# The norm's factor behind the products of the second block's stages

## The reference, cut to what matters

```python
def rms_norm_2(x, g):
    y = xf * lax.rsqrt(jnp.mean(xf * xf, axis=-1, keepdims=True) + EPS)
    return (y * g.astype(jnp.float32)).astype(x.dtype)

def second_block(x, ...):
    for l in range(DEPTH):
        h = rms_norm_2(x, norm1_g[l])
        z = h @ w_in[l]
        (cq, ckv, kpe, gq, gk, gv, glr, gr, su, gates) = split_in(z)
        ...
        x = x + merged @ w_out[l]
        h2 = rms_norm_2(x, norm2_g[l])
        x = x + jnp.square(jax.nn.relu(h2 @ w_ff1[l])) @ w_ff2[l]
```

## Time and profile before

| | |
|---|---|
| median of three runs | 2344.2 us (2341.02 to 2348.77) |
| profiled execution | 2345.54 us, span 2343.5 us |
| PE busy | 94% |
| PE weight loads | 89% |
| DVE busy | 71% |
| ACT busy | 60% |
| DMA, mean | 168 GB/s |

### The profile page before, as it was taken

The page is one execution under the profiler, slowest core; times in us unless marked ns, Lnnn a source line. Parts: engine busy times, 40 slices in busy tenths (PEclk is TensorE's granted clock), DMA queues, the critical chain, the costliest instruction groups (busy, mean ns, idle before and its releaser), DMA issues.

```text
span 2343.5 us, 42543 instructions
## 1 busy us (share of the span) xinstructions
PE 2200.8 (94%) x17524; PEld 2089.8 (89%) x17524; DVE 1656.4 (71%) x2998; ACT 1417.2 (60%) x2205; POOL 200.2 (9%) x178
## 2 busy tenths in 40 slices
PE   2989999999998999999999999899999989899999
PEld 2979899999998898999998987789999987799999
DVE  5898778678769887785879663647687663656653
ACT  2578887466546888854763557564543548564542
POOL 0000000022000000000231111000030111000000
PEclk9999999999999999999999999999999999999999
DMA  7555556567755564574655323245566323344553
GB/s 281 189 161 181 165 198 219 179 207 231 238 192 174 157 198 162 195 228 147 205 176 167 126 84 99 94 149 164 189 184 187 117 66 110 107 153 144 195 189 129
DMA packets 110593, 394.64 MB, mean 168 GB/s; under 512 B 12320, under 2 KB 13888, under 8 KB 110272
## 3 DMA queue, kind: packets, MB, share of 16 engines
q1 hardware_dynamic: 96768, 343.47, 45.3%
q0 software_dynamic: 11904, 43.03, 5.8%
q10 hardware_dynamic: 1728, 5.43, 0.6%
HBM read 390.83 MB, written 1.05 MB: 167 GB/s over the span
## 4 chain that ended last, share of the span: by engine, by line
PE 71%; DVE 14%; ACT 10%; issue 3%; DMA 1%; POOL 0%; SPq 0%; DVEq 0%; ACTq 0%
PE bank L550 69%; ACT scr L1046 4%; DVE WL L1554 3%; ACT WH L1046 3%; ACT L1035 2%; DVE arena L1618 2%; DMA ring<-in_w 1%; ACT arena L1046 1%; DVE arena L2252 1%; PE bank L630 1%; DVE scr L1601 1%; DVE scr L1801 1%; DVE arena L1726 1%; DVE scr L1788 0%; DVE small L1800 0%
## 5 line engine op out<-in xcount | busy, mean ns | idle before, releaser
L1046 ACT ACTIVATE WH<-ring 128x1024 fp32r<-128x1024 f32 (+1 forms) x638 | 669.8, 1052 | 729.3 <-PE bank L550 705.5
L550 PE MATMUL bank<-HTH,WH 128*128 128x256 f32 (+1 forms) x3408 | 981.7, 288 | 15.3 <-DVE HTL L1591 5.1
L550 PE MATMUL bank<-HTL,WH 128*128 128x256 f32 (+1 forms) x3408 | 965.0, 283 | 0.0
L550 PE MATMUL bank<-HTH,WL 128*128 128x256 f32 (+1 forms) x3408 | 964.0, 283 | 0.0
L1554 DVE TENSOR_TENSOR WL<-ring,WH 128x1024 fp32r<-128x1024 f32 (+2 forms) x602 | 731.2, 1223 | 198.3 <-ACT WH L1046 196.0
L550 PEld LDWEIGHTS bank<-HTH,WH 128*128 128x128 f32 (+1 forms) x3408 | 649.8, 191 | 28.9 <-issue 26.5
L550 PEld LDWEIGHTS bank<-HTL,WH 128*128 128x128 f32 (+1 forms) x3408 | 649.5, 191 | 4.0 <-issue 3.6
L550 PEld LDWEIGHTS bank<-HTH,WL 128*128 128x128 f32 (+1 forms) x3408 | 649.1, 190 | 0.1
L1035 ACT ACT_TABLE_LOAD x120 | 154.0, 1283 | 46.4 <-PE bank L550 28.5
L550 PE MATMUL bank<-ff2h,WH 128*128 128x256 f32 x512 | 144.0, 281 | 0.0
L550 PE MATMUL bank<-ff2l,WH 128*128 128x256 f32 x512 | 143.8, 281 | 0.0
(11 more groups left out here) (320 smaller groups left out, 3687.5 us busy)
## 6 DMA issues: line engine op xcount, KB each, us to landing
ring<-in_w SPq DMA_DIRECT2D x620, 512.0 KB, 4.0
arena<-in_wada POOLq DMA_DIRECT2D x80, 512.0 KB, 4.8
ring<-in_w SPq DMA_DIRECT2D x16, 384.0 KB, 3.8
arena<-in_wada SPq DMA_DIRECT2D x8, 512.0 KB, 19.5
arena<-in_wada ACTq DMA_DIRECT2D x8, 512.0 KB, 22.2
ring<-in_w SPq DMA_DIRECT2D x8, 288.0 KB, 2.8
XT<-in_xt SPq DMA_DIRECT2D x1, 1024.0 KB, 9.6
arena<-in_s POOLq DMA_DIRECT2D x4, 256.0 KB, 3.6
```

Of the source, the lines that this page charges most:

```text
L550: ins = e.matmul(out, a, b, start=(start and i == 0), stop=(stop and i == len(pairs) - 1))
L1046: return e.activation(out, a, func, **kw)
```

## The change

For the feed-forward stages 5 and 7 (`LATE`) both products run on the stream times gain alone. ACT writes `HTH` straight from `XT` once the last product of the stage before is done, DVE `HTL`. The two sums of squares stand ahead of the fifth unit, `factor` (1/(mean + eps)) is made by DVE at the seventh, and the residual multiplies by it.

For the mixer stages 4 and 6 (`RAW`) only the first three units (`su` but its last quarter) run on the raw stream. Its parts are made during the `res` groups of the stage before (chunks 6 and 7 at the boundary). PE runs the two sums behind chunk 3 of the opening. The normalised `HTH` chunk c is written when the opening has passed it (`opened`). The `su` results are evacuated by DVE, which multiplies three of four by `rstd`. The fill products are gone from these four boundaries. GpSimd's program is unchanged.

```diff
-        FREED_BY_VECTOR = {"xc", "ao", "so", "res", "up", "pe", "b0", "b1", "b2"}
+        FREED_BY_VECTOR = {"su", "xc", "ao", "so", "res", "up", "pe", "b0", "b1", "b2"}
...
             def boundary(st):
+                if st in LATE or st in RAW:
+                    return
...
             def chunk_ready(x, k):
                 l = x.group.l
+                if x.src == "h" and x.stage in RAW and x.i - plan.base[x.stage] < 3:
+                    return norm_vector("rawlo", x.stage, k)
...
+                    if xs[0].stage in RAW and xs[0].src == "h":
+                        st = xs[0].stage
+                        if k < 7:
+                            ins.then_inc(opened.inc("chunk", st, k), 1)
+                        if k == 3:
+                            for c in (6, 7):
+                                p.wait_ge(norm_scalar("sq", st, c))
+                                sums(c, square_tile(c), st, start=False)
...
+                if u - 4 in plan.base and plan.base.index(u - 4) in LATE:
+                    st = plan.base.index(u - 4)
+                    for c in (6, 7):
+                        p.wait_ge(norm_scalar("sq", st, c))
+                        sums(c, square_tile(c), st, start=False)
...
+            def raw_high(st, c):
+                p.wait_ge(residual_ready(st, c))
+                act(HTH[:, c, :], XT[:, c, :], ACT.Identity, scale=col("norm1_g_2", STAGES[st][1], c)).then_inc(
+                    norm_scalar.inc("rawhi", st, c), 1)
...
+                if st in LATE:
+                    p.wait_ge(unit_done(plan.closing[st - 1].end))
+                    for c in range(8):
+                        p.wait_ge(residual_ready(st, c))
+                        act(HTH[:, c, :], XT[:, c, :], ACT.Identity, scale=col("norm2_g_2", l, c)).then_inc(
+                            norm_scalar.inc("hi", st, c), 1)
+                    p.wait_ge(norm_vector("sq", st, 1))
+                    for c in (6, 7):
+                        act(square_tile(c), XT[:, c, :], ACT.Square).then_inc(norm_scalar.inc("sq", st, c), 1)
+                    return
...
+                if st in RAW:
+                    raw_high(st, 6)
+                    raw_high(st, 7)
...
+                if st in RAW:
+                    hi(units[plan.base[st] + 3])
...
                     p.wait_ge(norm_vector("t", st, c))
+                    if st in RAW:
+                        p.wait_ge(opened("chunk", st, c) if c < 7 else unit_done(plan.base[st] + 2))
...
+                    if st + 1 in RAW:
+                        raw_high(st + 1, 2 * gi)
+                        raw_high(st + 1, 2 * gi + 1)
...
                     else:
-                        ins = e.tensor_tensor(x, y, x, ALU.add)
+                        p.wait_ge(norm_vector("factor", st))
+                        serial(e.tensor_tensor(scaled[h], y, rstd, ALU.mult), ev_vector)
+                        ins = e.tensor_tensor(x, scaled[h], x, ALU.add)
...
+            def factor(st):
+
+                p.wait_ge(sums_done("sum", st, 7))
+                serial(e.tensor_scalar(rstd, bank[4][:, 0:T], 1.0 / 1024, 1e-6, ALU.mult, ALU.add), norm_vector)
+                e.reciprocal(rstd, rstd).then_inc(norm_vector.inc("factor", st), 1)
...
             def boundary(st):
+                if st in LATE:
+                    l = STAGES[st][1]
+                    raw_low(st, l, 0)
+                    raw_low(st, l, 1)
+                    residual(plan.closing[st - 1], l)
+                    for c in range(2, 8):
+                        raw_low(st, l, c)
+                    return
...
+                if st in RAW:
+                    raw_low_of("norm1_g_2", st, 6)
+                    raw_low_of("norm1_g_2", st, 7)
+                    lo(units[plan.base[st] + 3])
                 p.wait_ge(norm_scalar("rs", st))
...
+                if s == 0 and k == "su":
+                    p.wait_ge(norm_scalar("rs", st))
+                    if gi == 0:
+                        ins = e.tensor_tensor(SU[:, 0:2, :], v2(ps[:, :]), twice(rstd), ALU.mult)
+                    else:
+                        e.tensor_tensor(SU[:, 2, :], ps[:, 0:T], rstd, ALU.mult)
+                        ins = e.tensor_copy(SU[:, 3, :], ps[:, T:512])
+                    ins.then_inc(ev_vector.inc(k, l, gi, st), 1)
+                elif s == 2 and k == "res" and st + 1 in RAW and gi < 3:
+                    raw_low_of("norm1_g_2", st + 1, 2 * gi)
+                    raw_low_of("norm1_g_2", st + 1, 2 * gi + 1)
...
+                if u - 6 in plan.base and plan.base.index(u - 6) in LATE:
+                    factor(plan.base.index(u - 6))
```

More of the change, by code:

```diff
@@ L474, in program @@
         out_done = sig("out_done")
-        FREED_BY_VECTOR = {"xc", "ao", "so", "res", "up", "pe", "b0", "b1", "b2"}
+        opened = sig("opened")
+        FREED_BY_VECTOR = {"su", "xc", "ao", "so", "res", "up", "pe", "b0", "b1", "b2"}
         def bank_free(g):
@@ L1021, in norm_tile @@
             return scr[:, c // 2, T * (c % 2):T * (c % 2) + T]
+        LATE = (5, 7)
+        RAW = (4, 6)
         rstd = scr[:, 7, 0:T]
+        scaled = [scr[:, 7 + h, T:512] for h in range(2)]
         def scalar_program(e):
@@ L1085, in evac @@
                 ps, st = bank[g.bank], g.stage
-                plain = {"iq": (IQ, "pair"), "q": (Q, "pair"), "k": (K, "pair"), "su": (SU, "pair"), "gq": (GQ, "pair"),
+                plain = {"iq": (IQ, "pair"), "q": (Q, "pair"), "k": (K, "pair"), "gq": (GQ, "pair"),
                          "gk": (GK, "pair"), "ckv": (CKV, "pair"), "v": (VV, "tokens"), "gv": (GV, "tokens"),
@@ L1530, in scalar_program @@
                     evac(g, 1)
-                if u + 3 < len(units) and units[u + 3].split:
+                if u + 3 < len(units) and units[u + 3].split and not (u in plan.base and plan.base.index(u) in RAW):
                     hi(units[u + 3])
@@ L1571, in residual, with raw_low, raw_low_of @@
                     else:
-                        ins = e.tensor_tensor(x, y, x, ALU.add)
+                        p.wait_ge(norm_vector("factor", st))
+                        serial(e.tensor_tensor(scaled[h], y, rstd, ALU.mult), ev_vector)
+                        ins = e.tensor_tensor(x, scaled[h], x, ALU.add)
                     ins.then_inc(ev_vector.inc("res" if h else "half", l, g.gi, st), 1)
-            def boundary(st):
+            def raw_low(st, l, c):
+                p.wait_ge(norm_scalar("hi", st, c))
+                e.scalar_tensor_tensor(HTL[:, c, :], XT[:, c, :], col("norm2_g_2", l, c), HTH[:, c, :].bitcast(F32),
+                                       ALU.mult, ALU.subtract).then_inc(norm_vector.inc("lo", st, c), 1)
+            def raw_low_of(name, st, c):
+                p.wait_ge(norm_scalar("rawhi", st, c))
+                e.scalar_tensor_tensor(HTL[:, c, :], XT[:, c, :], col(name, STAGES[st][1], c),
+                                       HTH[:, c, :].bitcast(F32), ALU.mult, ALU.subtract).then_inc(
+                                           norm_vector.inc("rawlo", st, c), 1)
+            def factor(st):
+                p.wait_ge(sums_done("sum", st, 7))
+                serial(e.tensor_scalar(rstd, bank[4][:, 0:T], 1.0 / 1024, 1e-6, ALU.mult, ALU.add), norm_vector)
+                e.reciprocal(rstd, rstd).then_inc(norm_vector.inc("factor", st), 1)
+            def boundary(st):
+                if st in LATE:
[6 more added lines that the diff above has]
+                    return
                 if st:
@@ L1632, in evac @@
                     p.wait_ge(unit_done(g.end))
-                if s == 0 and k == "xc":
+                if s == 0 and k == "su":
[9 more added lines that the diff above has]
+                    raw_low_of("norm1_g_2", st + 1, 2 * gi + 1)
+                elif s == 0 and k == "xc":
                     c = 2 * gi
@@ L2127, in steps @@
                 def steps(r):
-                    p.wait_ge(ev_scalar("su", l, 0, 4 + 2 * l), ev_scalar("su", l, 1, 4 + 2 * l), L.G("bs", l))
+                    p.wait_ge(ev_vector("su", l, 0, 4 + 2 * l), ev_vector("su", l, 1, 4 + 2 * l), L.G("bs", l))
                     src = SU[32 * r:32 * r + 32, :, :].rearrange("p c (k i) -> p c k i", i=4)
@@ L2295, in vector_program @@
                 for v in (() if u in plan.opens else (u + 2, u + 3) if u + 1 in plan.opens else (u + 2,)):
+                    if v - 3 in plan.base and plan.base.index(v - 3) in RAW:
+                        continue
                     if v < len(units) and units[v].split and not units[v].pool:
```

## The result

| | before | after |
|---|---|---|
| median | 2346.7 us (13 runs, 2341.0 to 2349.1) | 2354.7 us (13 runs, 2349.0 to 2360.1) |
| after over before, 95% interval | | 1.0038 (1.0027 to 1.0048) |
| profiled execution, its span | 2343.5 us | 2351.5 us |
| mean granted clock of that execution | 0.986 | 0.982 |

The changed kernel is slower by 8.9 us of 2346.7 (6.3 to 11.3); the two medians and the two profiled spans differ by 8.0 each. That is the forecast direction, and inside its range, if only just: the forecast was 2351.3, the range ended at 2355, and the median is 2354.7. Of the 3.4 us between, 2.5 come from the kernel before, whose median over 13 runs is 2346.7 and not the 2344.2 of the three runs to which the sum was added.

What follows compares the result with a forecast made beforehand. TensorE, busy 94% of the span, was taken as the bound, so its idle stretches count. Terms +4.3 + 5.2 - 5.0 + 1.6 + 1.0 = +7.1 us on 2344.2 gave 2351.3 us, range 2348 to 2355.

Steps and rivals of the forecast that it cites:

- Part 1: Stage 4's opening: products start earlier, but sums of squares and hence the transposes come later, +4.3 us.
- Part 2: Stage 6's opening: as in stage 4, plus two multiplications in the closing residual; transposes later, +5.2 us.
- Part 3: Stages 5 and 7: first product 3.4 us earlier each, sums in the stream cost 0.9 each, -5.0 us.
- Part 4: Stage 3: four raw low parts queued on DVE delay PE's awaited last addition of squares, +1.6 us.
- Part 5: Kernel's end: the last residual, with two multiplications, takes 1.74 us instead of 0.76, +1.0 us.
- Part 6: Factor in stages 5 and 7, su evacuation moved to DVE: work hidden beside other work, cost 0.
- (a): Rival: later waits in stages 4 and 6 absorb half of 9.5 us; 2346.6, no change; chance 0.16.
- (b): Rival: memsets don't hold PE at the mixer openings, so they gain; -12.8 us, 2331.4; chance 0.07.
- (c): Rival: PE's clock falls to half around long waits and openings, 6.8 us more, 2358; chance 0.17.

Runs made afterwards that it cites:

- e3: The changed kernel with GpSimd's memsets released by the last product of the stage before, not by normalised chunk 7: 1.0010 of before, 2346.4 us.
- e1: Only the feed-forward part of the change (stages 5 and 7), on the kernel before: 0.9994 of before, 2342.5 us.
- e4: The kernel before with GpSimd's memsets released by the last product of the stage before: 1.0008 of before, 2344.5 us.
- e6: The kernel before with the transposes two units later in PE's order: 0.9957 of before, 2335.6 us.
- e9: The kernel before with early memsets and the transposes two units later in PE's order: 0.9945 of before, 2328.1 us.
- e10: Only the feed-forward part of the change, with early memsets and transposes two units later: 0.9943 of before, 2328.9 us.
- e12: e8 with feed-forward banks reordered, raw low parts behind the last addition of squares, first su evacuation ahead of unit 4's low part: 0.9877 of before, 2318.7 us.
- e8: The changed kernel with early memsets and the transposes two units later in PE's order: 0.9921 of before, 2327.3 us.
- e5: The changed kernel with 23 fill products ahead of PE's wait for the padded copies at stages 4 and 6: 1.0031 of before, 2352.0 us.
- e2: Only the mixer part of the change (stages 4 and 6), on the kernel before: 1.0054 of before, 2356.4 us.
- e7: The changed kernel with the transposes two units later in PE's order, memsets still late: 0.9968 of before, 2337.1 us.

## Why the prediction held, and where it was off

**Part 1, stage 4 (+4.3).** +4.27. The whole argument, that the release of the transposes hangs on the sums and these now stand behind 36 products, can be read link by link in the chain. The wait was to be 10.4 and is 10.26. That the memsets' release is the cause is shown by e3: take the memsets' wait away and the transposes come 5.13 us earlier.

**Part 2, stage 6 (+5.2).** +5.09; the four operations of the residual take 1.68 us (forecast 1.74).

**Part 3, stages 5 and 7 (-5.0).** -3.38 each at the first product (forecast 3.4) and +0.87 for the sums (0.9). ScalarE's copy with gain takes 0.51 us at a pitch of 0.4, as allowed for.

**Part 4, DVE in stage 3 (+1.6).** +1.56. It is shown twice: the stretch is 62.9 to 63.0 in before, e1, e4, e6, e9 and e10, 64.5 in every kernel with the raw low parts ahead of the addition, and 62.98 in e12, which has them behind it.

**Part 5, the end (+1.0).** +0.93.

**Part 6, the hidden work (0).** Nothing of it is on PE's path in after. One size and one premise weren't as taken. The factor's reciprocal of 128x256 (timeline of after) takes four times as long as a plain operation:

```profile
1656.42 0.42 DVE L1640 TENSOR_SCALAR scr<-bank 128x256 f32<-128x256 f32 x1
1656.87 1.75 DVE L1641 RECIPROCAL scr<-scr 128x256 f32<-128x256 f32 x1
```

The prediction said that the only reciprocal in the trace of before was that of 128x4. That was wrong. The groups by shape of before have two more (count, busy us, mean ns, idle ahead):

```profile
L1827 DVE RECIPROCAL small<-small 128x64 f32<-128x64 f32 x2 | 1.1, 553 | 0.1
L2049 DVE RECIPROCAL small<-small 128x16 f32<-128x16 f32 x2 | 0.5, 254 | 0.1
```

From 4 over 16 to 64 columns the time goes from 178 over 254 to 553 ns, some 6.25 ns a column; 256 columns come to 1.75 us by that, which is what was measured. So the size could have been read beforehand. Eight passes, as the Trainium skill has it (VectorE: DVE Perf Modes, "First, the fixed hardware budget"), were worked out as 3.4 us, twice too long; the 0.42 of a plain operation was four times too short. Neither changed the sum. And `su` at nothing rested on a cover, the wait for the transposes: e8 and e9 take the cover away, and PE then waits for it 0.36 us longer a stage with the change than without.

**The sum** was +7.1, the terms measure +6.8, and the 1.2 left over in the profiled execution fits the clock. Over all executions the half-speed time rose by 20.8 us, of which 16.3 are waiting in the profiled pair; the 4.5 left at 0.36 are 1.6 us, and 6.8 + 1.6 is 8.4, against 8.9 by the ratio and 8.0 by the medians.

**Rivals.** (a) The later waits took nothing in: PE's waits of over 1 us further down add up to 23.9 us in stage 4 and 24.9 in stage 6 of before, and to 23.4 and 25.2 in after. Single ones moved by up to 1 us, both ways. (b) was wrong not only in its condition but in its price. It let the transposes follow the opening at once if the memsets were early. e3 makes its condition true and gets 1.0010, not the -12.8 us: ScalarE's queue is next, with the eight scaled chunks and a weight split ahead of the copies. Having named one engine behind the wait I didn't follow the second one's program to the point at which it could have started. (c) was right in kind: the wait leaves the clock down, 0.53 and 0.63 behind it, and e3 and e5 each show an opening that fell to half speed. But the loss at the transposes grew by 0.5 us in stage 4 where I had put 1.7 for a doubled price (and by 0.1 in stage 6): in stage 4 the drop came 5.7 us before PE went on, and the lower level then lasted 4.5 us of work instead of the 3.4 of before at 1318.97. The Trainium skill (TensorE: Matmul & The Clock Gate, "HAM oscillation — how this bites in real kernels") warns of bursts with waits between; the trace agrees in that the clock fell inside both waits of 10.3 us, while behind those of 3.2 us in before it fell only when PE had gone on, 1.4 us after it in stage 4; and e5 shows that lifting it there is worth less than the intervals can tell.

## What to carry to other kernels

Before a factor is moved off an opening, list everything else that waits for the finished operand, side engines too: here a memset and two copies did, and an earlier opening only made their wait longer. Release a buffer by its last reader, not by whatever came last in the old order, and put independent units ahead of the step that waits; both together turned the same change from +8.9 us to about -5.6. A cost put at nothing because it lies under a wait has to be costed again as soon as that wait is worked on.

## What was not expected of the hardware

A reciprocal of 128x256 float32 on VectorE takes 1.75 us where a multiply-and-add takes 0.42. Openings after a wait of 1.9 us ran partly at half speed in some kernels (stage 6 of e3, 0.80, and of e5 and e7, 0.81) and at full speed in others with the same wait, as the window of e8 from that opening's first product on shows (71 products where e3 has 58); what decides it the runs don't tell.

```profile
1811.89:1820.64 8.75, 8.75 (x71) 8.64 (x71) 4.35 (x10) 4.42 (x10) 5.74 (x5) 1.00 0.27 91
```

And in before two operations of VectorE at stage 4's opening took far longer than their like, one of four columns and a weight split that takes 1.22 us in the mean (VectorE's timeline of before):

```profile
1309.99 3.64 DVE L1609 TENSOR_SCALAR small<-cols 128x4 f32<-128x4 f32 x1
1310.42 3.21 DVE L1554 TENSOR_TENSOR WL<-ring,WH 128x1024 fp32r<-128x1024 f32 x1
```

Both ended 0.02 us behind the second of GpSimd's memsets of 128x2048, which ran from 1310.06 on in steps of 1.8 us; the same weight split at 1315.05, beside a later memset, took its usual 1.23. The other runs show that the memsets are the cause. In the seven kernels that keep the late memsets (before, after, e1, e2, e5, e6, e7) the first of them starts 0.06 to 0.07 us behind the four-column operation, in stage 4 and in stage 6. In these 14 cases the operation took 3.6 us three times, 1.9 us eight times (until just behind the first memset's end) and 0.17 us three times. In the seven kernels with early memsets it took 0.15 to 0.17 us every time, and the split its usual 1.2, as here in e4 (DVE's timeline):

```profile
1305.84 0.16 DVE L1609 TENSOR_SCALAR small<-cols 128x4 f32<-128x4 f32 x1
1306.27 1.23 DVE L1554 TENSOR_TENSOR WL<-ring,WH 128x1024 fp32r<-128x1024 f32 x1 [0.27 <-ACT WH L1046]
```

The Trainium skill (SBUF — State Buffer, "Who interferes with whom") says that VectorE in its two-port modes and GpSimd lock each other out of a shared pair of ports, and that whoever issues first has the pair for the whole instruction. The trace agrees on the lock, if the four-column operation is the one locked out and the split stood behind it. It doesn't agree on the order or the length: the operation of VectorE has the earlier start, and it was held over two memsets here; whether the recorded start is the moment at which the ports are taken, no run shows. In before this was off PE's path. In stage 4 of e7 it wasn't: the `su` evacuation (DVE's timeline of e7) ended at 1320.49, 0.03 us behind the second memset, and PE waited 3.1 us for it.

```profile
1318.43 2.06 DVE L1716 TENSOR_TENSOR arena<-bank,scr 128x512 f32<-128x512 f32 x1
```
